# An encoder layer on one core: the third and fourth token sums of the gates moved out of attention, and the first two gate groups run side by side

## The reference

```python
u = rmsnorm(x, P['norm_mix'][l])
proj = u @ P['w_in'][l]                       # q, k, v, hyena, gates
q, k, v, hy, gates = jnp.split(proj, [o1, o2, o3, o4], axis=-1)
...
a = diff_attention(q, k, v, lam)              # 4 heads, w = softmax0 - lam * softmax1
a = rmsnorm(a, P['subln'][l]) * (1.0 - lam_init)
a = a.reshape(B, L, ATT_V_W) @ P['w_br_attn'][l]
...
hz = hz @ P['w_br_hyena'][l]
g = jax.nn.sigmoid(gates.astype(F32)).astype(x.dtype).reshape(B, L, N_BRANCH, D_MODEL)
x = x + (g[:, :, 0] * a + g[:, :, 1] * hz) @ P['w_out'][l]
```

## Time and profile before

| | |
|---|---|
| median of 3 runs | 2747.7 (2744.48 to 2748.73) |
| the profiled execution: its own time | 2748.03 |
| its span, on which all views of the profile count | 2746.2 |
| TensorE busy | 2640.7 (96%), 12283 matmuls |
| VectorE busy | 879.5 (32%) |
| ScalarE busy | 417.7 (15%) |
| GpSimd busy | 252.5 (9%) |
| matmuls of the gates, L1030 | 243.5, 896 of them |

### The profile page before, as it was taken

One profiled execution on the slowest core, in us unless ns is written; L12 is line 12 of the kernel. 1 busy time (PEld: TensorE's weight loads), 2 busy tenths in 40 slices (PEclk: granted clock), 3 DMA queues, 4 the chain that ended last, 5 costly groups with the idle time before them and its releaser, 6 DMA issues.

```text
span 2746.2 us, 29716 instructions
## 1 busy us (share of the span) xinstructions
PE 2640.7 (96%) x12283; PEld 1779.1 (65%) x12283; DVE 879.5 (32%) x1526; ACT 417.7 (15%) x946; POOL 252.5 (9%) x270
## 2 busy tenths in 40 slices
PE   7999899999989999999999999977999999999997
PEld 4554454466567777764455476547788788778876
DVE  5566723166773121134300044362111111111112
ACT  3120000144451101102100022110000000000002
POOL 0120100000001001042000002000110010011001
PEclk9999999999999999999999999978999999999999
DMA  4110211000001010041011100136787778778776
GB/s 156 31 50 11 80 54 31 0 1 16 1 24 47 24 46 24 24 168 31 31 46 46 61 31 24 69 123 250 245 270 256 263 256 281 252 244 271 255 263 245
DMA packets 189938, 315.78 MB, mean 115 GB/s; under 512 B 6122, under 2 KB 69951, under 8 KB 189216
## 3 DMA queue, kind: packets, MB, share of 16 engines
q1 hardware_dynamic: 181952, 292.87, 30.8%
q0 software_dynamic: 7904, 21.76, 3.1%
HBM read 288.40 MB, written 26.21 MB: 115 GB/s over the span
## 4 chain that ended last, share of the span: by engine, by line
PE 89%; DVE 8%; ACT 1%; issue 1%; DMA 0%; POOL 0%; POOLq 0%; DVEq 0%; SPq 0%; ACTq 0%
PE banks L748 60%; PE banks L1030 9%; PE banks L929 5%; PE banks L1119 4%; PE banks L1244 3%; PE banks L949 2%; PE banks L1378 2%; DVE arena L1895 2%; PE banks L964 1%; PE banks L764 1%; PE banks L1348 1%; DVE arena L1752 1%; DVE arena L2279 0%; DVE arena L2282 0%; DVE arena L2395 0%
## 5 line engine op out<-in xcount | busy, mean ns | idle before, releaser
L748 PE MATMUL banks<-arena 128*128 128x160 f32 (+3 forms) x8070 | 1754.3, 379 | 24.8 <-ACT arena L1449 7.9
L748 PEld LDWEIGHTS banks<-arena 128*128 128x128 f32 x8070 | 1247.0, 191 | 538.7 <-issue 480.3
L1030 PE MATMUL banks<-arena 128*128 128x320 f32 x896 | 243.5, 433 | 2.6 <-DVE arena L2031 2.1
L634 POOL TENSOR_TENSOR arena<-arena 128x512 f32<-128x512 f32 (+1 forms) x72 | 109.5, 1533 | 1303.7 <-DMA arena<-in_w_br_hyena 759.0
L1030 PEld LDWEIGHTS banks<-arena 128*128 128x128 f32 x896 | 169.8, 190 | 72.4 <-issue 2.3
L2360 DVE TENSOR_TENSOR arena<-arena,banks 128x160 f32<-128x160 f32 x128 | 41.2, 321 | 521.6 <-ACT arena L1679 489.2
L1679 ACT ACTIVATE arena<-banks 128x160 f32<-128x160 f32 x120 | 36.4, 304 | 764.4 <-PE banks L748 764.4
L929 PE MATMUL banks<-arena 128*128 128x512 f32 (+1 forms) x384 | 144.7, 527 | 2.5 <-DVE arena L1935 2.5
L1119 PE MATMUL banks<-arena 128*128 128x512 f32 x280 | 122.6, 593 | 0.7 <-ACT arena L1589 0.7
L1995 DVE TENSOR_REDUCE att<-banks 128x1 f32<-128x1024 f32 (+1 forms) x80 | 81.4, 1059 | 129.8 <-PE banks L949 129.7
L929 PEld LDWEIGHTS banks<-arena 128*128 128x128 f32 x384 | 71.4, 193 | 56.6 <-issue 53.7
(11 more groups left out here) (237 smaller groups left out, 1591.6 us busy)
## 6 DMA issues: line engine op xcount, KB each, us to landing
arena<-in_w_exp_gate SPq DMA_DIRECT2D x32, 2048.0 KB, 8.0
arena<-in_w_exp_up SPq DMA_DIRECT2D x32, 2048.0 KB, 12.9
arena<-in_w_exp_down SPq DMA_DIRECT2D x32, 2048.0 KB, 17.8
arena<-in_w_in SPq DMA_DIRECT2D x36, 512.0 KB, 4.1
arena<-in_x_prompt SPq DMA_DIRECT2D x8, 1024.0 KB, 8.0
residual_rows<-arena SPq DMA_DIRECT2D x10, 512.0 KB, 2.6
normed_rows<-arena SPq DMA_DIRECT2D x10, 512.0 KB, 2.6
arena<-residual_rows SPq DMA_DIRECT2D x5, 1024.0 KB, 14.7
```

Of the source, the lines that this page charges most:

```text
L634: done.inc(pool.tensor_tensor(out, l, r, op))
L748: last = pe.matmul(out, l, r, start=(n == 0), stop=(n == len(pairs) - 1))
L1030: last = pe.matmul(PS[:, 3 * (g % 2) + bank, 0:GN], l[:, k, :], r[:, k, :], start=(k == 0 and which in (G1, G2, G5)), stop=(k == 3), skip_ ...
```

## The change

On VectorE the sums 8 to 15 leave attention (units 32 to 37 held one each, 14 and 15 stood behind the last `output`). They go in two packs of four between the additions of the first gate groups. `UD3` and `UD4` change places: the pieces 8 to 11 are now `UD3`, 12 to 15 `UD4`. `G6` of group 0 waits for 8 sums, no longer for all 16; `G7` of group 0 waits for 12 and `G4` of group 0 for 16. On TensorE the products of groups 0 and 1 are written in a new order, with those that need neither `UD3` nor `UD4` first, and `sub_turn(6)` and `sub_turn(9)` stand next to each other. ScalarE's copies follow the new order, and the counts of the semaphores are adapted to it.

```diff
+        FIRST_DONE = {(0, G1): 1, (0, G2): 2, (0, G6): 3, (0, G5): 4, (1, G1): 5, (1, G2): 6, (1, G6): 7, (1, G5): 8,
+                      (0, G7): 9, (0, G4): 10, (0, G3): 11, (1, G7): 12}
...
+        FIRST_SUMS, FIRST_COPIES = [(1, 3, 4), (2, 5, 6)], [(1, 2, 4), (3, 5, 6)]
...
                 if which == G6:
-                    wait("gate_kept", 3 * g + 1)
+                    wait("gate_kept", gate_copied(g, 0))
+                    if g == 0:
+                        wait("act_sums", 8)
+                if which == G7:
+                    wait("gate_kept", gate_copied(g, 1))
+                    if g == 0:
+                        wait("act_sums", 12)
+                if which == G4:
+                    wait("gate_kept", gate_copied(g, 2))
                     if g == 0:
                         wait("act_sums", 16)
...
             values(UNITS - 1)
             gate_product(0, G6)
             gate_product(0, G5)
-            gate_product(0, G7)
             wait("wt_ready", W_HEAD * HEADS)
             gate_product(1, G1)
-            gate_product(0, G4)
+            gate_product(1, G2)
             wait("o_ready", UNITS)
             sub_turn(0)
+            gate_product(1, G6)
+            gate_product(1, G5)
+            gate_product(0, G7)
+            sub_turn(3)
+            gate_product(0, G4)
             gate_product(0, G3)
-            sub_turn(3)
-            gate_product(1, G2)
             sub_turn(6)
-            gate_product(1, G6)
             sub_turn(9)
-            gate_product(1, G5)
             gate_product(1, G7)
...
-            for g in range(GATES):
-                if g:
-                    kept(g, 0, G1)
-                    sigmoid_rest(g - 1)
+            kept(0, 1, G6)
+            kept(1, 0, G1)
+            kept(0, 2, G7)
+            sigmoid_22(0)
+            sigmoid_rest(0)
+            kept(1, 1, G6)
+            kept(1, 2, G7)
+            sigmoid_22(1)
+            for g in range(2, GATES):
+                kept(g, 0, G1)
+                sigmoid_rest(g - 1)
                 kept(g, 1, G6)
...
                 out, l, r = ((UD1[:, k, :], u12, u11), (UD2[:, k, :], u22, UD1[:, k, :]),
-                             (UD4[:, k, :], u21, UD2[:, k, :]), (UD3[:, k, :], u22, u12))[kind]
+                             (UD3[:, k, :], u22, u12), (UD4[:, k, :], u21, UD2[:, k, :]))[kind]
...
-                if 32 <= u < 38:
-                    act_sum(u - 24)
                 mixed(u)
             output(UNITS - 2)
             output(UNITS - 1)
-            act_sum(14)
-            act_sum(15)
             dve.wait_ge(sem["o_ready"], UNITS)
...
             gate_11(0)
+            gate_11(1)
+            for n in range(8, 12):
+                act_sum(n)
+            attended(0)
             gate_22(0)
-            attended(0)
+            for n in range(12, 16):
+                act_sum(n)
+            attended(3)
             gate_12(0)
-            attended(3)
-            gate_11(1)
             attended(6)
             attended(9)
             gate_22(1)
```

More of the change, by code:

```diff
@@ L396, in seven_done, with gate_summed, gate_copied @@
             return early[which] if g == 0 else 5 + 7 * (g - 1) + which + 1
+        FIRST_DONE = {(0, G1): 1, (0, G2): 2, (0, G6): 3, (0, G5): 4, (1, G1): 5, (1, G2): 6, (1, G6): 7, (1, G5): 8,
+                      (0, G7): 9, (0, G4): 10, (0, G3): 11, (1, G7): 12}
         def gate_done(g, which):
-            return seven_done(g, which, GATES)
+            return FIRST_DONE.get((g, which)) or seven_done(g, which, GATES)
+        FIRST_SUMS, FIRST_COPIES = [(1, 3, 4), (2, 5, 6)], [(1, 2, 4), (3, 5, 6)]
+        def gate_summed(g, n):
+            return FIRST_SUMS[g][n] if g < 2 else 3 * g + n + 1
+        def gate_copied(g, n):
+            return FIRST_COPIES[g][n] if g < 2 else 3 * g + n + 1
         PAIRS = NT // 2
@@ L1015, in gate_product @@
                 if which == G2 and g >= 2:
-                    wait("gate_sum", 3 * (g - 2) + 1)
+                    wait("gate_sum", gate_summed(g - 2, 0))
                 if which == G5 and g >= 2:
-                    wait("gate_sum", 3 * (g - 2) + 3)
+                    wait("gate_sum", gate_summed(g - 2, 2))
                 if which == G6:
-                    wait("gate_kept", 3 * g + 1)
+                    wait("gate_kept", gate_copied(g, 0))
[7 more added lines that the diff above has]
+                    wait("gate_kept", gate_copied(g, 2))
                     if g == 0:
                         wait("act_sums", 16)
[L1023 to L1026, removed]
                 if which == G3:
-                    wait("gate_sum", 3 * g + 2)
+                    wait("gate_sum", gate_summed(g, 1))
                 for k in range(4):
@@ L1550, in kept @@
                 if g >= 1:
-                    act.wait_ge(sem["gate_sum"], 3 * (g - 1) + (1, 3, 2)[i])
+                    act.wait_ge(sem["gate_sum"], gate_summed(g - 1, (0, 2, 1)[i]))
                 act.copy(KEPT[i], PS[:, 3 * (g % 2), 0:GN]).then_inc(sem["gate_kept"], 1)
@@ L1556, in sigmoid_22 @@
                 t1, t2 = gate_cols(n)
-                act.wait_ge(sem["gate_sum"], 3 * g + 2)
+                act.wait_ge(sem["gate_sum"], gate_summed(g, 1))
                 act.activation(gates_of[:, 1, t2], gates_of[:, 1, t2], ACT.Sigmoid).then_inc(sem["gate_sig"], 1)
@@ L1566, in sigmoid_rest @@
                 act.activation(gates_of[:, 1, t1], PS[:, 3 * (g % 2), 0:GN], ACT.Sigmoid).then_inc(sem["gate_sig"], 1)
-                act.wait_ge(sem["gate_sum"], 3 * g + 3)
+                act.wait_ge(sem["gate_sum"], gate_summed(g, 2))
                 both = gates_of[:, 0, :].rearrange("p (s c) -> p s c", s=2)[:, :, t1]
@@ L2028, in act_sum @@
                     dve.wait_ge(sem["qk_mm"], 5 * (HEADS - 1))
+                if n == 8:
+                    dve.wait_ge(sem["qk_mm"], 5 * HEADS)
                 if n == 12:
-                    dve.wait_ge(sem["qk_mm"], 5 * HEADS)
+                    dve.wait_ge(sem["s_mm"], 2 * UNITS)
                 acts.inc(dve.tensor_tensor(out, l, r, ALU.subtract))
@@ L2070, in gate_11 @@
                 dve.wait_ge(sem["gate_mm"], gate_done(g, G2))
-                dve.wait_ge(sem["gate_kept"], 3 * g + 1)
+                dve.wait_ge(sem["gate_kept"], gate_copied(g, 0))
                 if 1 <= g // 2 < KD - 1:
@@ L2078, in gate_22 @@
                 dve.wait_ge(sem["gate_mm"], gate_done(g, G5))
-                dve.wait_ge(sem["gate_kept"], 3 * g + 3)
+                dve.wait_ge(sem["gate_kept"], gate_copied(g, 2))
                 dve.tensor_tensor(SG[g // 2][:, 1, t2], PS[:, 3 * (g % 2) + 2, 0:GN], KEPT[2], ALU.add).then_inc(sem["gate_sum"], 1)
```

## The result

The changed kernel is slower. Two comparisons with the kernel before were made, each with its own runs of both: the ratio is 1.0048 (95% interval 1.0033 to 1.0064; medians 2758.02 and 2747.54, 8 runs each) and, later on another occasion, 1.0065 (1.0051 to 1.0079). The first ratio on 2747.5 is +13 us, the two medians differ by 10.5; the forecast was +12.2. The runs of the kernel before alone spread from 2738.6 to 2748.7, so an effect of this size is read from the trace, and the times can only confirm it roughly. The profiled execution's span went from 2746.2 to 2755.3.

What follows compares the result with a forecast made beforehand. TensorE, with 89% of the chain that ended last, was taken as the bound. Terms -1.1 - 2.1 + 7.1 + 3.7 + 0.3 + 4.3 were summed to +12.2, giving 2760.0 us; range 2753 to 2764.5.

Steps and rivals of the forecast that it cites:

- attention (A): Attention units: removing six sums gains 1.1, 0.7 at 782.28 and 0.4 at 792.97; the other four were hidden.
- first stand: First transposes, step 2: TensorE waits 7.5 for the copy of `attended(0)` behind the first pack, 0.4 before; +7.1.
- the turns with GpSimd: First pack: VectorE's sums and GpSimd's weight additions each wait for the other's whole operation, ending the pack 3.1 later.
- second stand: Behind `G7` of group 0: sums held behind `gate_22(0)` make TensorE stand 4.1, 0.4 before; +3.7.
- side by side: `sub_turn(6)` and `sub_turn(9)` without a product between them: 1.1 of waiting in three places instead of 2 x 0.4; +0.3.
- the clock: TensorE behind both new stands: granted clock falls to 0.50, costing 2.1 each, +4.3 in all, bounds 0 and 6.8.
- The first products: Four gate products ahead of the first transposes: take 8.8, end about 834.0, scalings at 833.84, so transposes start with nothing lost.
- The third fall: Rival: clock falls again in the stretch of `sub_turn(6)` and `sub_turn(9)`, costing 1.7 to 2.6 more, 2762; chance 0.1.
- No turns: Rival: sums and GpSimd don't take turns at the first pack; price -3.1, time 2757; chance 0.12.
- The clock stays high: Rival: behind the new stands the clock stays at its upper level or falls once, 2755.7 to 2758; chance 0.15.
- Swallowed later: Rival: a later wait not tied to TensorE, such as a weight load, absorbs the gates' loss, 2748; chance 0.04.
- That the change does what it says: Rival: VectorE finishes the sums inside the products and TensorE meets no new stand, 2744.8; chance 0.03.

Runs made afterwards that it cites:

- e5: Kernel before, with only `G6` of group 0 waiting for 8 sums and `G7` of group 0 for all 16; ratio to before 0.9990.
- e3: Changed kernel, with GpSimd starting its weight sums of block 1 only once VectorE has 12 token sums; ratio to the kernel before 1.0047.
- e4: Changed kernel, with idle matmuls on TensorE inside both stands, ahead of the third and sixth transposing steps; ratio to the kernel before 1.0036.
- e1: Changed kernel, with `attended(0)` ahead of `gate_11(1)` and the first pack, and the second pack ahead of `gate_22(0)`; ratio to the kernel before 1.0008.
- e2: Changed kernel, with only `attended(0)` moved ahead of `gate_11(1)` and the first pack; second pack left in place; ratio to the kernel before 1.0029.
- e6: Changed kernel, with only the second pack moved ahead of `gate_22(0)`; ratio to the kernel before 1.0025.
- e10: The changed kernel measured once more, nothing altered; ratio to the kernel before 1.0065.
- e8: Changed kernel, with sums 8 to 11 in attention units 33, 35, 36, 37, 12 to 15 behind `attended(0)` and `gate_11(1)`, `sub_turn(6)` between `G4` and `G3`; ratio to before 0.9988.
- e9: Kernel before with `G6` waiting for 8 sums, `G7` for 16, sums 8 to 11 in units 33, 35, 36, 37, and 12 to 15 ahead of the roots; ratio 0.9992.
- e7: Changed kernel's order of products and copies, with sums 8 to 13 back in attention and 14, 15 behind `attended(0)` and `gate_11(1)`; ratio to before 1.0001.

## Why the prediction was right, point by point

| step | forecast | measured in the profiles |
|---|---|---|
| attention (A) | -1.1 | -0.5 |
| the wait of `G6` | -2.1 | -2.1 here; S -2.4 in e5 |
| first stand, less 0.41 | +7.1 | +6.7 |
| of it, the turns with GpSimd | 3.1 | 2.8 (e3) |
| second stand, less 0.41 | +3.7 | +3.8 |
| side by side, and all else in S | +0.3 | +0.5, as what is left of S |
| the clock | +4.3 | +5.3; S -5.2 in e4 |
| sum | +12.2 | +13.7 |

The measured terms are those of single profiles. The forecast of 2760.0 for the whole execution stands 2.0 above the median, though the stretch rose by 1.5 more than the sum said. So the close hit of the total owes something to the spread of the executions; the terms are the better test. In the sum itself two clock terms of 2.1 make 4.2, not 4.3.

**The stands.** The reading that decided was VectorE's list of instructions: four sums stood ahead of a copy for which TensorE waits, and TensorE runs in order. e1, e2 and e6 show that VectorE's order is the cause of the stands: with both packs moved, 0.41 and 1.15 are left of them. For the second stand it is the place behind `gate_22(0)` that counts, as the prediction said.

**The first products.** The prediction had the transposes start with nothing lost. They waited 0.23 for the scaling (827.24) and lost the overlap with the products besides. The transposes that stand together lost the same once more at 859.29. This is what the row "all else in S" holds.

**The turns.** The row at 792.97 gave the right size. The first three sums of the pack have a GpSimd operation before them and take 1.74 to 1.78; the fourth found GpSimd done.

**The clock.** The 5.3 are 2.7 and 2.1 on the matmuls behind the stands, against e4's, and twice 0.25 on the transposing steps that end them. Both stands brought it down, as the rows with 7.91 and 3.65 had the earlier trace rows. The 2.1 each was somewhat low: 5.87 and 4.69 worked at half make 2.9 and 2.3. How much a stand costs by the clock was partly luck, as the last section shows. The third fall, behind the transposes that stand together, didn't come in any of the profiles. The prediction's argument against it was incomplete, though. The earlier trace rows show that transposes raised the clock at 20.63; a little later, in the kernel before, the clock fell again among transposes of the same kind, with gaps of 0.97 and 0.96 between them:

```profile
24.90 1.16 PE L764 MATMUL banks<-ident_sb,arena 128*128 128x128 f32 x8 [0.97 <-DVE arena L1752]
27.02 1.93 PE L764 MATMUL banks<-ident_sb,arena 128*128 128x128 f32 x8 [0.96 <-DVE arena L1752]
```

The granted clock is 0.51 in the window 27.00:30.40 there. So a stretch of transposes with gaps can bring the clock down; the one at 857.2 to 861.2, with waits of 0.41, 0.22 and 0.41, kept it at 1.00. The rule that the prediction names from the Trainium skill (page "TensorE: Matmul & The Clock Gate", section "Part 4: PE-mode transpose"), that a transpose doesn't count as busy in the way of a matmul, is at odds with the rise at 20.63 and fits the fall at 27.0, and no fall of the kind it would have made came here.

**Attention.** Right in one unit and wrong in the other. In the unit of the earlier trace rows at 782.28 the 0.7 came. In the unit at 792.97 I took the sum out of GpSimd's way and forgot that the mixing operation behind it (L2014, two inputs in SBUF, too) then comes into it. It was in part there already in the kernel before, which the prediction did not read (1.79 in place of 1.28):

```profile
794.93 1.79 DVE L2014 SCALAR_TENSOR_TENSOR arena<-arena,att 128x1024 f32<-128x1024 f32 x1
```

That unit took 6.21 from its first maxima to the next before, takes 6.41 now, and 5.67 in e1. The changed kernel, e10, e4, e6, e8 and e9 all show it. Timelines of GpSimd and VectorE in that unit, first of the changed kernel, then of e1:

```profile
783.69 5.19 POOL L645 TENSOR_TENSOR arena<-arena 128x512 f32<-128x512 f32 x4 [455.62 <-DMA arena<-in_w_br_hyena]
...
787.62 2.35 DVE L2036 SCALAR_TENSOR_TENSOR arena<-arena,att 128x1024 f32<-128x1024 f32 x1
```

```profile
785.22 6.24 POOL L645 TENSOR_TENSOR arena<-arena 128x512 f32<-128x512 f32 x4 [457.04 <-DMA arena<-in_w_br_hyena]
...
789.05 1.28 DVE L2036 SCALAR_TENSOR_TENSOR arena<-arena,att 128x1024 f32<-128x1024 f32 x1
```

The same operation takes 2.35 or 1.28. In e1 to e3 it came first and GpSimd waited (6.24 for its four in e1, in place of 5.19). Which engine is first hangs on less than a tenth of a microsecond. Counted from the first maxima of unit 32, GpSimd, which waits for a load, starts at 11.59 to 11.65 in the six profiles with an A of 37.4, and at 11.69 to 11.83 in the three with 36.7. Whether this goes with the program or with the execution is not shown; both profiles of the changed kernel have 11.62.

**The rivals.** No turns: refuted by e3. The clock stays high: refuted, and priced by e4. A third fall: not seen. Swallowed later: refuted by the 313.4 of gates that both kernels show, by the time from there to the end (1570.6 before, 1572.2 now), and by the ratio. That the change does what it says: it does for its wait (e5), and loses far more beside it.

## What to carry to other kernels

Relax a wait by changing its count before moving the work that it waits for: here that edit takes 2.4 off S (e5, a gain that the times can't tell from none), and the whole change loses 13.7. Work that is moved off one engine's path must not land ahead of something for which another engine waits, nor behind a wait that holds it until then, on any engine that runs in order; look for a place where the engine is idle anyway (here the exponential's wait in attention and the wait for the roots). A stand of TensorE can cost more than its length: behind those of 7.1 and 4.2 the products ran at half clock for some microseconds and took 1.1 to 2.7 longer. A pack of VectorE additions beside GpSimd additions makes both slow, here 6.19 in place of 3.39 and 6.37 in place of 5.17.

## What the runs showed of the hardware

**The clock makes equal programs differ ahead of the change.** Up to unit 32 of attention all these kernels are the same program, but its first maxima in that unit start between 769.1 (e8) and 778.3 (before) in the profiles. Windows over one early stretch (columns as above; PEld is the loading of weights), first of before and then of the changed kernel:

```profile
400.00:440.00 40.00, 35.02 (x101) 19.12 (x100) 16.11 (x27) 1.54 (x3) 0.00 (x0) 0.91 0.35 105
```

```profile
400.00:440.00 40.00, 35.02 (x110) 19.43 (x109) 16.86 (x28) 1.04 (x3) 0.00 (x0) 1.00 0.33 103
```

In before the granted clock fell twice in this stretch, to 0.91 in the mean, and in the changed kernel it stayed at 1.00, at the same busy time of 35.02, in which it got through more matmuls (110 records against 101, though some can be missing). So a difference of some microseconds between two single spans says nothing here, and this is why the span of the changed kernel rose by 9.1 only while the stretch around the change rose by 13.7. Up to unit 32 it is 6.2 ahead of before; behind the gates it takes 1.6 more, and its low clock there lasts 3.4 longer. I had read the stretch at 774.60 to 778.00 as the price of a stand, which it is; but whether a short stand brings such a fall varies from run to run (it is in before, e3, e6 and e9, and not in the other profiles).

The stand of 2.9 at 264.80, which the prediction took as one that leaves the clock high, is such a case. Windows behind it, first of before and then of the changed kernel:

```profile
267.70:271.10 3.40, 3.40 (x8) 1.36 (x8) 3.30 (x6) 1.17 (x2) 2.41 (x2) 1.00 0.00 0
```

```profile
267.90:271.30 3.40, 3.40 (x5) 1.33 (x4) 3.29 (x6) 1.17 (x2) 1.60 (x2) 0.50 0.00 0
```

The clock fell behind this same stand in the changed kernel, e2, e3, e4, e7 and e8, and stayed high in the six other profiles.

**The same stand has no fixed price.** Behind the second stand, 4.21 in four of the profiles, the 16 matmuls took 6.55 (the changed kernel), 6.16 (e3) and 5.59 (e2), against 4.47 at full clock.
